# Decaying eight sequences' states on GpSimd instead of ScalarE, and three weight splits one unit later on VectorE

## The reference

```
xn = rmsnorm(h);  z = xn @ w_in                      # (tokens, 1024) @ (1024, 3592)
y_a = z_B * causal_conv3(z_C * z_H)                  # short convolution group
q, k, v = silu(causal_conv4(z_qkv)); q, k = l2norm(q), l2norm(k)
per head (4) and chunk:  S = S * exp(g_last) + k_dec^T v_new    # gated delta rule, S is 128 x 128
                         v_new = u - w S;  o = q_dec S + (qk) v_new
y_b = rmsnorm(o) * silu(z_gate)
h = h + concat(y_a, y_b) @ w_out
h = h + relu(rmsnorm(h) @ w_up)^2 @ w_down;  y = rmsnorm(h)
```

## Time and profile before

| | us |
|---|---|
| median of 3 runs (lowest to highest) | 1265.84 (1264.52 to 1266.84) |
| the profiled execution's own time | 1266.84 |
| its span, first to last instruction | 1265.0 |
| PE busy in the span | 1244.9 |
| DVE busy | 808.5 |
| POOL busy | 654.7 |
| ACT busy | 462.9 |

### The profile page before, as it was taken

One profiled execution on the slowest core, in us unless ns is written; L12 is line 12 of the kernel. 1 busy time (PEld: TensorE's weight loads), 2 busy tenths in 40 slices (PEclk: granted clock), 3 DMA queues, 4 the chain that ended last, 5 costly groups with the idle time before them and its releaser, 6 DMA issues.

```text
span 1265.0 us, 23661 instructions
## 1 busy us (share of the span) xinstructions
PE 1244.9 (98%) x9592; PEld 1210.5 (96%) x9592; DVE 808.5 (64%) x1272; ACT 462.9 (37%) x794; POOL 654.7 (52%) x503
## 2 busy tenths in 40 slices
PE   7999999999999999999999999999999999999997
PEld 6999999899999999999999999999999999999997
DVE  6455898536564666646987666565667658566456
ACT  6565654321222213224232333333434433333303
POOL 2422120111121212214889898887889989788701
PEclk9999999999999999999999999999999999999999
DMA  6222673743323323231144344443745452542003
GB/s 203 55 72 75 173 208 76 214 121 92 93 68 97 96 60 94 85 101 35 41 169 165 144 140 151 145 155 127 257 141 205 170 167 72 204 137 70 18 18 121
DMA packets 164717, 152.86 MB, mean 121 GB/s; under 512 B 21095, under 2 KB 141315, under 8 KB 161922
## 3 DMA queue, kind: packets, MB, share of 16 engines
q1 hardware_dynamic: 141634, 138.49, 33.9%
q10 hardware_dynamic: 22976, 12.88, 3.7%
HBM read 104.05 MB, written 47.29 MB: 120 GB/s over the span
## 4 chain that ended last, share of the span: by engine, by line
PE 92%; DVE 3%; issue 2%; POOL 1%; DMA 1%; ACT 1%; SPq 0%; POOLq 0%; DVEq 0%; ACTq 0%
PE banks L2251 15%; PE banks L2254 15%; PE banks L2253 15%; PE banks L1712 11%; PE banks L1714 11%; PE banks L1713 11%; PE banks L2298 1%; PE banks L2299 1%; PE banks L2300 1%; PE banks L2182 1%; PE banks L1898 1%; DMA w_raw<-in_w_in 1%; DVE hT L3144 1%; PE banks L2306 1%; PE banks L1891 1%
## 5 line engine op out<-in xcount | busy, mean ns | idle before, releaser
L1712 PE MATMUL banks<-xn_high,w_high 128*128 128x384 f32 (+1 forms) x672 | 227.5, 339 | 0.9 <-DVE xn_low L2396 0.8
L1714 PE MATMUL banks<-xn_high,w_low 128*128 128x384 f32 (+1 forms) x672 | 219.2, 326 | 0.0
L1713 PE MATMUL banks<-xn_low,w_high 128*128 128x384 f32 (+1 forms) x672 | 219.1, 326 | 0.0
L959 POOL TENSOR_TENSOR w_low<-w_raw,w_high 128x1024 fp32r<-128x1024 f32 x30 | 76.6, 2552 | 231.1 <-ACT w_high L1226 231.1
L2251 PE MATMUL banks<-op_high,set_high 128*128 128x264 f32 x672 | 191.4, 285 | 0.2
L2254 PE MATMUL banks<-op_high,set_low 128*128 128x264 f32 x672 | 191.0, 284 | 0.0
L2253 PE MATMUL banks<-op_low,set_high 128*128 128x264 f32 x672 | 190.6, 284 | 0.0
L3144 DVE TENSOR_TENSOR hT<-hT,banks 128x528 f32<-128x528 f32 x148 | 100.7, 700 | 106.5 <-PE banks L2254 106.0
L1109 POOL TENSOR_TENSOR set_low<-w_up_raw,set_high 128x512 fp32r<-128x512 f32 x79 | 122.6, 1553 | 60.1 <-ACT set_high L1541 60.1
L2251 PE MATMUL banks<-up_high_T,set_high 128*128 128x264 f32 x496 | 141.7, 286 | 1.0 <-POOL up_low_T L1116 0.6
L2254 PE MATMUL banks<-up_high_T,set_low 128*128 128x264 f32 x496 | 141.0, 284 | 0.0
(11 more groups left out here) (394 smaller groups left out, 3048.6 us busy)
## 6 DMA issues: line engine op xcount, KB each, us to landing
op_raw<-ops_kept SPq DMA_DIRECT2D x21, 1056.0 KB, 4.9
w_up_raw<-in_w_up SPq DMA_DIRECT2D x16, 1024.0 KB, 5.6
ops_kept<-u_rows SPq DMA_DIRECT2D x28, 528.0 KB, 2.8
w_raw<-in_w_in SPq DMA_DIRECT2D x28, 512.0 KB, 4.2
ops_kept<-u_T SPq DMA_DIRECT2D x42, 264.0 KB, 2.1
w_down_half<-in_w_down SPq DMA_DIRECT2D x3, 2048.0 KB, 8.9
w_down<-in_w_down SPq DMA_DIRECT2D x24, 256.0 KB, 4.1
w_raw<-in_w_out SPq DMA_DIRECT2D x8, 512.0 KB, 4.1
```

Of the source, the lines that this page charges most:

```text
L959: pool.tensor_tensor(w_l[n % 2][:, :, :], w_raw[n % 2][:, :, :], w_h[n % 2][:, :, :].bitcast(F32), ALU.subtract).then_inc(w_low, 1)
L1712: pe.matmul(bank[:, 0:w], w_h[n % 2][:, k, :], hi[:, c0:c0 + w], start=(k == first), stop=False)
L1713: pe.matmul(bank[:, 0:w], w_h[n % 2][:, k, :], lo[:, c0:c0 + w], start=False, stop=False)
L1714: ins = pe.matmul(bank[:, 0:w], w_l[n % 2][:, k, :], hi[:, c0:c0 + w], start=False, stop=(k == last))
```

## The change

ACT's `decay_states` goes away: 32 instructions of 128 x 128. GpSimd gets one of its own: four instructions, one a head, each a product of 128 x 1024 elements with `eg_seq` as a second operand that is broadcast along 128 columns. They stand in GpSimd's stream at unit 40, ahead of the split for tile 15, and wait for `sample_made` alone.

The condition `g == (n == LOW_BY_DVE[0])` of VectorE's stream is 1 for n = 9 and 0 for n = 10 to 13; now it is 1 for all. So the splits for tiles 11, 12, 13 and 14 move from the head of units 30, 33, 36 and 39 to the head of units 31, 34, 37 and 40. The split for tile 10 stays.

```diff
--- before.py
+++ after.py
@@ -1035,6 +1035,12 @@
                 for i in range(2):
                     pool.tensor_copy(wq_part(1, i), sequences(qf[:, :, 0:NS], i)).then_inc(q_beside, 1)
 
+            def decay_states(h):
+
+                pool.wait_ge(sample_made, 1)
+                sh = SSs[h // 2][:, h % 2, :, :]
+                pool.tensor_tensor(sh, sh, eg_seq[:, :, h:h + 1].to_broadcast([P, NSEQ, P]), ALU.mult).then_inc(ss_decayed, 1)
+
             def pick_column():
                 pool.memset(pick[:, :], 0.0).then_inc(pick_set, 1)
                 pool.memset(ssr[:, :], 0.0).then_inc(pick_set, 1)
@@ -1073,6 +1079,9 @@
                     if u == TILE0["k"]:
                         zero_sample_rows()
                         beside()
+                    if u == TILE0["use"]:
+                        for h in range(NH):
+                            decay_states(h)
                     if u == TILE0["states"]:
                         power(0)
                     if s == 3 and t >= 2:
@@ -1408,14 +1417,6 @@
                 act.activation(wq_part(0, 0), sequences(made, 0), ACT.Copy, scale=-1.0)
                 act.activation(wq_part(0, 1), sequences(made, 1), ACT.Copy, scale=-1.0).then_inc(w_kept, 1)
 
-            def decay_states(h):
-
-                act.wait_ge(sample_made, 1)
-                for b in range(NSEQ):
-                    sh = SSs[h // 2][:, h % 2, b, :]
-                    ins = act.activation(sh, sh, ACT.Copy, scale=eg_seq[:, b, h:h + 1])
-                ins.then_inc(ss_decayed, 1)
-
             def o_square(t):
 
                 c = rows(t)
@@ -1436,8 +1437,6 @@
                 if u == TILE0["v"]:
                     act.wait_ge(norms_done, 2)
                     keep_v_scaled(0)
-                if TILE0["sample"] < u <= TILE0["sample"] + NH:
-                    decay_states(u - TILE0["sample"] - 1)
                 if u == TILE0["next"]:
                     o_square(0)
                     load_solved(1)
@@ -2889,7 +2888,7 @@
                 kind, i, _ = IN_TILES[n]
                 for g in range(3):
                     u = 3 * n + g
-                    if g == (n == LOW_BY_DVE[0]) and n in LOW_BY_DVE:
+                    if g == 1 and n in LOW_BY_DVE:
                         split_low(n + 1)
                     if kind == "H":
                         evict_h(n, g)
```

## The result

| | before | after |
|---|---|---|
| median, us (lowest to highest) | 1265.38 (1264.52 to 1266.84), 4 runs | 1275.34 (1273.17 to 1275.70), 4 runs |
| ratio, 95% interval | | 1.0074 (1.0056 to 1.0092) |
| profiled execution, its span | 1266.84, 1265.0 | 1274.39, 1272.6 |
| mean granted clock | 0.997 | 0.995 |

The account below looks back on a forecast made before the run. PE was taken to bound the kernel. 1.0 us (later splits) + 8.6 (DVE held) + 2.0 (slow clock) = 11.6 us on the profiled 1266.84, or 1277.4 us against the median of 1265.84; range 1271 to 1284.

Parts of the forecast that it names:

- What bounds the kernel: PE, busy 1244.9 of 1265.0 us; shortening ACT's or DVE's work gains at most a few tenths of a us.
- Part 1: Later splits alone: tile 13's ends at 213.3, PE wants it at 212.34 and waits 1.0 us; tiles 11, 12, 14 cost 0.
- Part 2: States on GpSimd: 9.8 us of ACT work removed for no gain; four GpSimd products of 2.4 us each added.
- GpSimd's products start when L2035 ends, and in turns with DVE: Products start at 208.09 us and alternate, one instruction each, with DVE's solve of unit 36 and tile 13's split.
- Each holds DVE for 2.14 us, 8.6 in all: At unit 36's solve and tile 13's split, four holds bring PE's wait to 1.0 + 8.6 = 9.6 us.
- The slow clock: TensorE's clock falls during the wait at tile 13, and dense products behind it lose 2.0 us, between 0 and 4.2.
- What follows the wait: Behind tile 13, the ws_qs copy, tile 14's split and SP's w_raw load come later but cost 0, PE being late itself.
- Sum: Whole kernel: 1.0 + 8.6 + 2.0 = 11.6 us slower, 1277.4 us against the median.
- The signs: Profile after: PE wait of 9 to 10 us, four steps near 2.5 us, tile 13's split starting near 220.7.
- DVE not held: At unit 36's solve, GpSimd's products do not hold DVE; only 1.0 us is lost, 1266.8 us; chance 11%.
- Longer products: GpSimd's state products take 3.2 us each, DVE loses 3.3 us more, 1280.7 us (1287 at twice 2.4); chance 8%.
- Faster: Freeing ACT's 9.8 us removes PE's longest wait behind the start, 1.6 us, giving 1264.2; 2% for anything faster than that.

Follow-up runs that it names:

- part2_late: Kernel before with the states on GpSimd, splits unmoved, the four products also waiting for the end of tile 0's solve: 1266.58 us, ratio 0.9999.
- pe_busy: Changed kernel with 16 idle products (128x208) on TensorE ahead of the wait for tile 13's split: 1272.63 us, ratio 1.0055.
- one_head: Changed kernel's order of splits, but only the last head's states on GpSimd, the other three on ScalarE: 1269.57 us, ratio 1.0023.
- two_heads: Kernel before, splits unmoved, with the states of heads 2 and 3 on GpSimd, heads 0 and 1 on ScalarE: 1269.53 us, ratio 1.0021.
- part2: Kernel before with only the states moved to GpSimd, the splits where they were: 1273.17 us, ratio 1.0061.
- tile13_back: Changed kernel with tile 13's split alone back at the head of unit 36: 1273.07 us, ratio 1.0052.
- stores_late: Kernel before, nothing moved to GpSimd, with SyncE's store of X waiting until ScalarE has decayed two heads: 1270.52 us, ratio 1.0028.
- late: Changed kernel with the four GpSimd products also waiting for the end of tile 0's solve: 1267.58 us, ratio 1.0005.

## Why the prediction was right, step by step

- **What bounds the kernel.** Right. The end moved by what TensorE waited plus the clock, 9.4 of 9.96 us, and ScalarE's 8.8 us less of busy time gave nothing.
- **Part 1, 1.0 us at tile 13, 0 elsewhere.** Right: 0.8 us of wait as the row counts it, and the tile's first product 1.04 us later behind L2035 (7.25 us against 6.21), a ratio of 1.001, and no wait for the splits of tiles 11, 12 and 14 in after.
- **Part 2 removes 9.8 us of ACT for nothing.** Right, shown by part2_late: the time of the kernel before.
- **GpSimd's products start when L2035 ends, and in turns with DVE.** Right: they start at 206.40, 208.2 in the time of before, and four steps are held, one for each.
- **Each holds DVE for 2.14 us, 8.6 in all.** The mis-sized term: 1.60 us each and 6.4 in all, 2.2 us too much. I took the subtraction of two full tiles for the nearest row and allowed the broadcast operand only to make it dearer (3.2 us, a lower end of 2.37). It makes it cheaper, 1.91 us alone against the 2.4 assumed, and no rival stood for shorter products. With a full operand the holds come to 8.2 us, near the forecast's 8.6. The size that the prediction takes to the letter from the Trainium skill's rule (SBUF — State Buffer, section SBUF: two separate sides), 9.5 us, was too high twice: by the duration, and by the 0.2 to 0.3 us by which each hold is shorter than the instruction.
- **The slow clock, 2.0 us.** 2.24 us by the trace; pe_busy shows it to be a term of its own. That the size came so near is luck in part, since 2.0 was picked between 0 and 4.2. The forecast did not say how long a wait brings the slow clock; one_head shows one of 2.4 us that doesn't.
- **What follows the wait costs 0.** Right for the change as it is, with the reason given (TensorE itself is late). I had not seen how near the stores of the solve stand to the loads of round 1: by the table under two_heads, the kernel before has about 1 us of slack there (18.4 against some 17 to 18, an estimate). My expectations for part2 and tile13_back, the time of before, failed on it by 7 us. That a load lands late because of SP's stores and weight loads is shown by stores_late; which of these transfers does it was not taken apart.
- **Sum.** 11.6 forecast; 0.8 + 6.4 + 2.2 = 9.4 read, 9.96 measured. The signs held in kind and not in size, all for the one term: the wait was 7.2 us and not 9 to 10, the held steps 1.97 and not 2.5, and the split started at 218.5 in the time of before and not at 220.7.
- **The rivals.** DVE not held: excluded by the four steps and by late. Longer products: excluded, they are shorter. Faster: excluded by part2_late.

No version of these beat the kernel before.

## What to carry to other kernels

Work moved from ScalarE to GpSimd isn't free because ScalarE was busy: while GpSimd runs with SBUF operands, count one VectorE instruction of two SBUF inputs held for each GpSimd instruction, for nearly that one's whole length, and ask what stands behind VectorE in that stretch. Others can be held too: in late, a `TENSOR_SCALAR` (`L2828`) that takes 0.47 us elsewhere took 1.02 beside the last product. If something does, start GpSimd's work at an event behind the critical stretch (here the end of the solve, which took 7 us back to none) rather than splitting it finer. And when a stage ends late, look not only at who consumes its result but also at the stores and loads queued behind it, and at whose transfers they will then meet.

## What the runs showed of the hardware that I had not expected

- A GpSimd product of 1024 elements a partition with a factor broadcast along its inner 128 takes 1.91 us alone (late) and holds DVE for 1.60 us; with a full second operand it holds for 2.02 to 2.11.
- Halved instructions hold it 0.73 each: 5.8 us for the same work, against 6.4 whole.
- The granted clock stayed up behind a wait of 2.4 us in one place (one_head) and was at 0.50 behind one of 1.9 us in another (stores_late), so the length of the wait alone doesn't tell.
- SP's two stores of 512 KB and the two weight loads behind them, moved by some 3 us, nearly doubled the landing time of ScalarE's loads, the first of which is issued 10.8 us after the first store. Issues in stores_late, against 2.9 and 3.3 us in the kernel before:
```profile
At<-At_kept ACTq DMA_DIRECT2D x1, 256.0 KB, 5.3
X<-X_kept ACTq DMA_DIRECT2D x1, 256.0 KB, 5.8
```
